# Four outputs at a time behind the norms of a two-block transformer kernel: four PSUM banks, weights in slices of two rows of tiles, and a re-timed norm chain

## The chip, the cores and the metric

The kernel runs on 1 core of one Trainium2 chip. The metric is the device time of one execution in microseconds (us). Before the change three runs gave 2636.99, 2637.52 and 2639.55 us, so the median is 2637.52 us.

## The reference, cut to what matters

Two transformer blocks of two layers each work on one sequence of 512 tokens with 1024 channels, in fp32. The change touches the second block only:

```python
def second_block(x, ...):
    for i in range(2):                                    # DEPTH = 2
        h = rms_norm_2(x, attn_pre_norm[i])
        z = h @ w_in[i]                                   # 1024 -> 26 tiles of 128 columns and 8 gate columns
        ...                                               # dilated attention, convolution mixer, gated delta rule
        x = x + rms_norm_2(mix @ w_out[i], attn_post_norm[i])      # post norm 0
        h = rms_norm_2(x, ffn_pre_norm[i])
        f = (silu(h @ w_gate[i]) * (h @ w_up[i])) @ w_down[i]      # 2816 hidden = 22 tiles
        x = x + rms_norm_2(f, ffn_post_norm[i])                    # post norm 1
    return x

def rms_norm_2(x, gain):
    return x * rsqrt(mean(x * x, axis=-1) + 1e-6) * gain
```

So each post norm is followed at once by a pre norm and a product of the new `x` with a large weight.

## The kernel before, in words

All activations are held transposed: 128 channels on the partitions, 512 tokens along the free dimension, so `x` is 8 tiles of 128x512 (`x_sb`; KD = 8). A product of fp32 accuracy is made of three matmuls of a rounded type: every fp32 operand is split into a high part (`whi`, `h_hi`) and the rest (`wlo`, `h_lo`), and a tile of output sums `h_hi*whi + h_lo*whi + h_hi*wlo` over the 8 tiles k of the input, 24 matmuls of 128x128 by 128x512.

**Units, pairs and slots.** One output tile is a *unit*; two units are a *pair*. There are two weight slots, s = 0 and 1, each with a `raw`, a `whi` and a `wlo` buffer of 8 (or 11) tiles of 128x128, and one PSUM bank each (ACC = banks 0 and 1). For unit (v, s) the SP queue loads `raw[s]` (line 458) once `wlo` of the unit before in this slot has been made; ScalarE makes `whi[s]` (`hi_next`, line 1449) when the matmuls that used the old one are done; VectorE makes `wlo[s]` (`low`, line 2095); TensorE computes it (`unit`, line 622); VectorE empties the bank. Numbers in semaphores (`w_hi_ready`, `w_lo_ready`, `unit_done`, `acc_free`) count the units of the whole program. The order on each engine is the order in which the code is written; nothing is scheduled by a planner.

**A post norm** (`post_norm` on ScalarE and VectorE, `post_parts` on GpSimd). The last pair of the output product leaves 8 tiles `y`. Their squares are summed on VectorE into `prod`, except the last, which stays in `cv1`; TensorE sums both over the channels with a matrix of ones (lines 1398 and 1400). ScalarE loads the table for logarithm and exponential (line 1460), and makes 1/rms by `exp(-0.5*ln(...))` (lines 1453, 1456) into a PSUM bank. Then for each of the 8 tiles n: VectorE scales `y` (line 2773) and adds it to `x` (2776); ScalarE makes `h_hi = x*gain` (2017), and the square of `x` (2008); VectorE makes `h_lo` (2767) for tiles 0, 2, 4, 6, 7, and GpSimd (546) from a copy in `pad` (2015) for tiles 1, 3, 5. GpSimd also sums the squares (554). The pre norm's 1/rms (`rstd`) is not needed before the matmuls: it is applied to their outputs. So the next product can start with tile k = 0 as soon as that is there.

**The product behind it** is `stream_pair` (line 686): for each k it issues 3 matmuls for the output in slot 0 and 3 for the one in slot 1. Before k = 7 `post_norm_sum` (lines 708, 710, 712) sums the squares over the channels in three fp32 matmuls. Behind it come plain units again. It is used at three places: the first pair of the gate/up product behind post norm 0 in both layers, and the first pair of layer 1's in-projection behind post norm 1 of layer 0. Layer 0's in-projection, behind the last product of the first block, uses `first_pair` (line 641). Post norm 1 of layer 1 is the end of the program; its tiles are turned (1428) and stored.

In the in-projection VectorE empties a bank with `project(i)` (2405), and turns outputs 0 to 3 by position with `rotary(i)` (2445 to 2448), for which TensorE makes a partner (`partners`, 1017).

## Time and profile before

| what | value |
|---|---|
| median of 3 runs | 2637.52 us (2636.99 to 2639.55) |
| the profiled execution | 2636.79 us, its span 2635.0 us |
| granted TensorE clock, mean | 0.989 of full |
| TensorE busy | 2551.0 us, 97% of the span |
| VectorE busy | 1514.5 us, 57% |
| ScalarE busy | 1105.3 us, 42% |
| GpSimd busy | 134.1 us, 5% |
| DMA | 208.04 MB, 79 GB/s in the mean |

The engines are PE (TensorE), PEld (its weight loads, which overlap PE), DVE (VectorE), ACT (ScalarE), POOL (GpSimd) and SP (the queue that issues most DMAs). A matmul's recorded length is longer than the distance to the next one, since matmuls are pipelined, so a busy PE can still be one that could do more; distances between starts tell its pace. A granted clock of 1.00 is TensorE's level of 2.4 GHz, 0.50 that of 1.2 GHz. "Idle before <-releaser" names what ended a wait.

### The profile page before, as it was taken

To read this page: it belongs to the slowest core of one execution; us is meant where nothing else is said; L and a number is where in the kernel's file an instruction comes from. 1 tells how busy PE (TensorE), PEld (TensorE's weight loads), DVE (VectorE), ACT (ScalarE), POOL (GpSimd) and SP (SyncE) were. 2 spreads that over 40 slices of the span, in tenths; PEclk is the share of its full clock that TensorE was granted. 3 is DMA by queue.
4 is the path that set the end of the run, shared out by engine and by line. 5 is a ranking of instruction groups with operands and counts; after the bars stand their busy time and mean duration, and the time that the engine had idled before them with its cause. 6 is when DMAs were issued, how large, how long until landed. Compare 5 with 4: busy or idle time off the path is not lost.

```text
span 2635.0 us, 36784 instructions
## 1 busy us (share of the span) xinstructions
PE 2551.0 (97%) x12956; PEld 2021.1 (77%) x12966; DVE 1514.5 (57%) x1957; ACT 1105.3 (42%) x1602; POOL 134.1 (5%) x119
## 2 busy tenths in 40 slices
PE   7999999999999999999998899999899999899998
PEld 5767888887668888887678778888676787688886
DVE  4656755756556746656975554344559755543444
ACT  4554433435554424432475443232424754431323
POOL 1000000000000000000212010000102120100000
PEclk9999999999999999999999999999999999999998
DMA  4203332333113333342220223333221201233333
GB/s 133 72 1 89 98 108 87 99 93 93 49 33 92 102 93 96 100 115 64 56 65 11 64 77 104 91 96 106 55 77 52 65 18 56 72 101 90 96 99 92
DMA packets 394592, 208.04 MB, mean 79 GB/s; under 512 B 9738, under 2 KB 392660, under 8 KB 394484
## 3 DMA queue, kind: packets, MB, share of 16 engines
q1 hardware_dynamic: 391396, 202.79, 26.7%
q0 software_dynamic: 2176, 3.06, 0.5%
q8 instruction: 65, 1.06, 0.2%
q10 hardware_dynamic: 912, 0.77, 0.1%
q14 instruction: 43, 0.35, 0.0%
...
## 4 chain that ended last, share of the span: by engine, by line
PE 89%; DVE 6%; ACT 3%; issue 1%; DMA 0%; SPq 0%; DVEq 0%; ACTq 0%
PE ps L622 65%; PE ps L641 6%; PE ps L899 2%; DVE ps L2773 1%; DVE x_sb L2776 1%; ACT whi L1449 1%; PE ps L1052 1%; PE ps L1067 1%; DVE yc L2497 1%; DVE h_lo L2767 1%; PE ps L1227 1%; PE ps L954 1%; PE ps L1205 1%; PE ps L956 1%; PE ps L955 1%
## 5 line engine op out<-in xcount | busy, mean ns | idle before, releaser
L1449 ACT ACTIVATE whi<-raw 128x1024 fp32r<-128x1024 f32 (+1 forms) x354 | 395.8, 1119 | 1071.2 <-PE ps L622 947.5
L622 PE MATMUL ps<-h_hi,whi 128*128 128x512 f32 x1984 | 789.2, 398 | 4.7 <-ACT whi L1449 4.1
L622 PE MATMUL ps<-h_lo,whi 128*128 128x512 f32 x1984 | 773.7, 390 | 0.0
L622 PE MATMUL ps<-h_hi,wlo 128*128 128x512 f32 x1984 | 530.3, 389 | 0.0
L2095 DVE TENSOR_TENSOR wlo<-raw,whi 128x1024 fp32r<-128x1024 f32 (+1 forms) x354 | 458.7, 1296 | 56.2 <-ACT whi L1449 55.1
L622 PEld LDWEIGHTS ps<-h_hi,whi 128*128 128x128 f32 x1984 | 373.3, 188 | 89.7 <-ACT whi L1449 8.2
L622 PEld LDWEIGHTS ps<-h_lo,whi 128*128 128x128 f32 x1984 | 373.2, 188 | 82.7 <-issue 6.2
L622 PEld LDWEIGHTS ps<-h_hi,wlo 128*128 128x128 f32 x1984 | 372.5, 188 | 77.2
L622 PE MATMUL ps<-a_hi,whi 128*128 128x512 f32 x592 | 230.3, 389 | 0.0
L622 PE MATMUL ps<-a_lo,whi 128*128 128x512 f32 x592 | 230.3, 389 | 0.0
L2808 DVE TENSOR_TENSOR cv<-ps,rstd 128x512 f32<-128x512 f32 x88 | 60.9, 692 | 248.9 <-PE ps L622 241.0
L622 PE MATMUL ps<-a_hi,wlo 128*128 128x512 f32 x592 | 152.4, 389 | 0.0
L2321 DVE TENSOR_TENSOR pad<-ps,rstd 128x512 f32<-128x512 f32 x88 | 61.0, 693 | 130.6 <-PE ps L622 118.4
L622 PEld LDWEIGHTS ps<-a_lo,whi 128*128 128x128 f32 x592 | 111.1, 188 | 23.1
L622 PEld LDWEIGHTS ps<-a_hi,wlo 128*128 128x128 f32 x592 | 111.1, 188 | 23.1
L622 PEld LDWEIGHTS ps<-a_hi,whi 128*128 128x128 f32 x592 | 111.1, 188 | 23.0
L2284 DVE TENSOR_TENSOR x_sb<-x_sb,ps 128x512 f32 (+1 forms) x40 | 27.5, 687 | 110.1 <-PE ps L622 94.1
L2330 DVE SCALAR_TENSOR_TENSOR cv<-pad,pc,cv 128x512 f32<-128x512 f32 x88 | 66.1, 751 | 11.0
L2497 DVE SCALAR_TENSOR_TENSOR yc<-ypad,pd,yc 128x512 f32<-128x512 f32 x88 | 70.4, 841 | 1.6
L1694 ACT ACTIVATE cv<-pad,pc,pb 128x512 f32<-128x512 f32 x88 | 70.5, 802 | 0.1
L1706 ACT ACTIVATE a_hi<-prod 128x512 f32 (+1 forms) x44 | 27.9, 633 | 97.8 <-DVE prod L2337 97.8
L641 PE MATMUL ps<-a_hi,whi 128*128 128x512 f32 x176 | 68.5, 389 | 0.0
...
## 6 DMA issues: line engine op xcount, KB each, us to landing
...
```

What stands on the lines that cost most here:

```text
L622: return pe.matmul(ps[:, ACC[s], :], w[s][:, k, :], r[:, k, :], start=start, stop=stop)
L641: return pe.matmul(ps[:, ACC[s], :], w[s][:, k, :], r[:, k, :], start=start, stop=stop)
L899: pe.matmul(ps[:, TRN[h % 2], :], vaug[:, h // GROUP, h % 2, kt, :], probs[:, kt, :], start=(kt == 0), stop=(kt == TB - 1)).then_inc(PV_do ...
L1449: act.activation(whi[s][:, 0:kt, :], raw[s][:, 0:kt, :], ACT.Copy).then_inc(w_hi_ready.sem, 1)
L1694: act.activation(cv[s][:], pad[s][:, 1:SEQ + 1], ACT.Identity, scale=param(pb, L, 2 * NF + col), bias=param(pc, L, 2 * NF + col))\
L1706: act.activation(tile(a_hi, j), prod[:], ACT.Copy).then_inc(ahi_ready.sem, 1)
L2095: dve.tensor_tensor(wlo[s][:, 0:kt, :], raw[s][:, 0:kt, :], whi[s][:, 0:kt, :].bitcast(F32), ALU.subtract).then_inc(w_lo_ready.sem, 1)
L2284: dve.tensor_tensor(tile(x, n), tile(x, n), ps[:, ACC[s], :], ALU.add).then_inc(acc_free.sem, 1)
L2321: dve.tensor_tensor(pad[s][:, 1:SEQ + 1], ps[:, ACC[s], :], rstd[:], ALU.mult).then_inc(acc_free.sem, 1)
L2330: dve.scalar_tensor_tensor(cv[s][:], pad[s][:, 2:SEQ + 2], param(pc, L, col), cv[s][:], ALU.mult, ALU.add)\
L2497: ins = dve.scalar_tensor_tensor(yc[:, t, :], src, w, yc[:, t, :], ALU.mult, ALU.add)
L2808: dve.tensor_tensor(cv[s][:], ps[:, ACC[s], :], rstd[:], ALU.mult).then_inc(acc_free.sem, 1)
```

## The change

`wide_pairs` takes the place of `stream_pair` at its three places and of `first_pair` in layer 0's in-projection. It computes four outputs at once in the PSUM banks WIDE = ACC[0], ACC[1], TRN[1], STAT[1], that is the work of two pairs: for each k 12 matmuls instead of 6. A slot's 8 tiles of 128 columns then hold 2 input tiles k by 4 outputs instead of 8 input tiles by 1 output: slot 0 holds k = 0, 1, slot 1 k = 2, 3, then slot 0 is refilled with k = 4, 5 and slot 1 with k = 6, 7. The refills fall into the post norm: on ScalarE behind tiles 3 and 6, on VectorE behind tile 5 and at the end, followed by the cast of the next pair's slot 0. Loads are changed to match: for the in-projection one DMA a slot, for gate and up two, of which ScalarE waits for the first with a semaphore of its own.

The chain of the post norm is changed too. In post norm 0 the table load is left out (the table in place holds the functions), and the last square is read from PSUM instead of from `y`, the copy waiting for it. In post norm 1 the table load is moved ahead of the last square. VectorE makes `h_lo` of tile 0 before it adds tile 1. GpSimd sums all 8 squares, so that one matmul instead of three makes the pre norm's sum, before k = 6 instead of k = 7.

Behind it, the first two pairs of gate/up have an epilogue of their own (`first_silus`, `first_pairs`), and in the in-projection four `project` stand together, followed by a cast and the two `rotary`; the two `partners` on TensorE follow the wide pairs.

```diff
+        WIDE = (ACC[0], ACC[1], TRN[1], STAT[1])
@@ SP: loads
+                    if off == OFF_UP2[0]:
+                        for k in range(0, KD, 2):
+                            load_wide(BASE2 + L * PAIRS2 + off + k // 4, (k // 2) % 2,
+                                      two_keys(wv["w_gate_2"], L, k, 2), two_keys(wv["w_up_2"], L, k, 2))
+                        pairs(2, n)
+                    elif off == 0:
+                        for k in range(0, KD, 2):
+                            load_wide(BASE2 + L * PAIRS2 + k // 4, (k // 2) % 2, two_keys(wv["w_in_2"], L, k, 4))
...
@@ GpSimd: post_parts
                 post_square_sum(p, 5)
+                post_square_sum(p, 6)
+                post_square_sum(p, 7)
@@ TensorE
+            def wide_pairs(v, wait_rhs, before, columns, done):
+                for k in range(KD):
+                    slot, pair = (k // 2) % 2, v + k // 4
+                    before(k)
+                    if k == 0:
+                        pe.wait_ge(acc_free.sem, v * 2 + 2)
+                    if k % 2 == 0:
+                        pe.wait_ge(w_lo_ready.sem, pair * 2 + (slot + 3))
+                    wait_rhs(k, 0)
+                    for o in range(4):
+                        bank, w = ps[:, WIDE[o], :], 4 * (k % 2) + columns[o]
+                        pe.matmul(bank, whi[slot][:, w, :], h_hi[:, k, :], start=k == 0, stop=False)
+                        pe.matmul(bank, whi[slot][:, w, :], h_lo[:, k, :], start=False, stop=False)
+                        mm = pe.matmul(bank, wlo[slot][:, w, :], h_hi[:, k, :], start=False, stop=k == KD - 1)
+                        if k == KD - 1 and o < 3:
+                            mm.then_inc(done.sem, 1)
+                    if k % 2 == 1:
+                        mm.then_inc(unit_done.sem, 1)
             def post_norm_sum(p):
-                pe.wait_ge(pssq_done.sem, pssq_done.at(p, KD - 4))
-                pe.matmul(ps[:, STAT[0], :], ones[:], ssq[:], start=True, stop=False)
-                pe.wait_ge(psq_ready.sem, psq_ready.at(p, KD - 2))
-                pe.matmul(ps[:, STAT[0], :], ones[:], sqt[:, 0, :], start=False, stop=False)
-                pe.wait_ge(psq_ready.sem, psq_ready.at(p, KD - 1))
-                pe.matmul(ps[:, STAT[0], :], ones[:], sqt[:, 1, :], start=False, stop=True).then_inc(stat_ready.sem, 1)
+                pe.wait_ge(pssq_done.sem, pssq_done.at(p, KD - 2))
+                pe.matmul(ps[:, STAT[0], :], ones[:], ssq[:], start=True, stop=True).then_inc(stat_ready.sem, 1)
...
-                stream_pair(V + OFF_UP2[0], h_hi, h_lo, need_post(2 * L), lambda k: k == KD - 1 and post_norm_sum(2 * L))
+                wide_pairs(V + OFF_UP2[0], need_post(2 * L), lambda k: k == KD - 2 and post_norm_sum(2 * L), (0, 2, 1, 3), wide_up)
@@ ScalarE: last_post_squares
-                    post_square(i, v, PAIRS_O - 1, 1)
+                    if i == 1:
+                        logs_and_exps()
+                    if i == 0:
+                        act.wait_ge(unit_done.sem, v * 2 + 4)
+                        act.wait_ge(yssq_done.sem, yssq_done.at(L, KD - 3))
+                        act.activation(cv[1][:], ps[:, ACC[1], :], ACT.Square).then_inc(ysq_ready.sem, 1)
+                        gates_in(0, 1)
+                    else:
+                        post_square(i, v, PAIRS_O - 1, 1)
                     hi_next(v + 1, 1, KD)
                 def post_rstd(i):
-                    logs_and_exps()
@@ ScalarE: post_norm
+                        if n == 3:
+                            wide_high(v + 1, 0)
+                        if n == 6:
+                            wide_high(v + 1, 1)
+                    hi_next(v + 2, 0, KD)
+                    act.wait_ge(stat_ready.sem, stat_ready.at(gen, 0))
+                    order.settle()
+                    order.told(rs(rstd[:], ps[:, STAT[0], :], DM), rstd_ready, gen, 0)
@@ VectorE: post_norm
+                        if more and n == 1:
+                            post_low(0)
                         order.settle()
                         order.told(dve.tensor_tensor(x[:, n, :], x[:, n, :], scaled, ALU.add), x2_ready, L, i * KD + n)
-                        if more and n - 1 in LOW_DVE:
+                        if more and n > 1 and n - 1 in LOW_DVE:
                             post_low(n - 1)
+                        if more and n == 5:
+                            low(v + 1, 0, KD)
                     if more:
                         post_low(KD - 1)
+                        low(v + 1, 1, KD)
+                        low(v + 2, 0, KD)
```

On ScalarE, at the end of the output product before post norm 0, this stood in a row before (`cv0`, `cv1` are the squares of the last two tiles of `y`, `whi0` and `whi1` the next weights):

```order
L1449 ACTIVATE whi0<-raw0 128x1024
L1977 ACTIVATE cv0<-y_sb 128x512
L1977 ACTIVATE cv1<-y_sb 128x512
L1449 ACTIVATE whi1<-raw1 128x1024
L1460 ACT_TABLE_LOAD
L1453 ACTIVATE lnt<-ps,eps 128x512
L1456 ACTIVATE ps<-lnt 128x512
```

and this stands there now:

```order
L1487 ACTIVATE whi0<-raw0 128x1024
L2019 ACTIVATE cv0<-y_sb 128x512
L2041 ACTIVATE cv1<-ps 128x512
L1487 ACTIVATE whi1<-raw1 128x1024
L1491 ACTIVATE lnt<-ps,eps 128x512
L1494 ACTIVATE ps<-lnt 128x512
```

The table load is gone, and the last square reads PSUM; the cast into `whi1` still stands between that square and the logarithm.

On VectorE, from tile 4 to the end of post norm 0, this stood in a row before:

```order
L2773 SCALAR_TENSOR_TENSOR ps<-y_sb,gains,ps 128x512
L2776 TENSOR_TENSOR x_sb<-x_sb,ps 128x512
L2767 SCALAR_TENSOR_TENSOR h_lo<-x_sb,gains,h_hi 128x512
L2773 SCALAR_TENSOR_TENSOR ps<-y_sb,gains,ps 128x512
L2776 TENSOR_TENSOR x_sb<-x_sb,ps 128x512
L2773 SCALAR_TENSOR_TENSOR ps<-y_sb,gains,ps 128x512
L2776 TENSOR_TENSOR x_sb<-x_sb,ps 128x512
L2767 SCALAR_TENSOR_TENSOR h_lo<-x_sb,gains,h_hi 128x512 x2
L62 ISA
L2808 TENSOR_TENSOR cv0<-ps,rstd 128x512
```

and from the same point (the add of tile 5 with its `h_lo` of tile 4) this stands there now:

```order
L2877 TENSOR_TENSOR x_sb<-x_sb,ps 128x512
L2866 SCALAR_TENSOR_TENSOR h_lo<-x_sb,gains,h_hi 128x512
L2180 TENSOR_TENSOR wlo0<-raw0,whi0 128x1024
L2872 SCALAR_TENSOR_TENSOR ps<-y_sb,gains,ps 128x512
L2877 TENSOR_TENSOR x_sb<-x_sb,ps 128x512
L2872 SCALAR_TENSOR_TENSOR ps<-y_sb,gains,ps 128x512
L2877 TENSOR_TENSOR x_sb<-x_sb,ps 128x512
L2866 SCALAR_TENSOR_TENSOR h_lo<-x_sb,gains,h_hi 128x512 x2
L2180 TENSOR_TENSOR wlo1<-raw1,whi1 128x1024
L2180 TENSOR_TENSOR wlo0<-raw0,whi0 128x1024
L62 ISA
L2944 TENSOR_TENSOR cv0<-ps,rstd 128x512
```

The refill of slot 0 stands in the middle of the norm, that of slot 1 and the cast for the unit behind the wide pairs at its end.

On TensorE, around the sum of squares for the pre norm, this stood in a row before (behind k = 6, ahead of k = 7):

```order
L686 MATMUL ps<-h_hi,wlo0 128x512
L686 MATMUL ps<-h_hi,whi1 128x512
L686 MATMUL ps<-h_lo,whi1 128x512
L708 MATMUL ps<-ssq,ones 128x512
L710 MATMUL ps<-sqt,ones 128x512
L712 MATMUL ps<-sqt,ones 128x512
L686 MATMUL ps<-h_hi,whi0 128x512
```

and this stands there now (behind k = 5, ahead of k = 6):

```order
L740 MATMUL ps<-h_hi,whi0 128x512
L741 MATMUL ps<-h_lo,whi0 128x512
L742 MATMUL ps<-h_hi,wlo0 128x512
L751 MATMUL ps<-ssq,ones 128x512
L740 MATMUL ps<-h_hi,whi1 128x512
L741 MATMUL ps<-h_lo,whi1 128x512
```

One sum took the place of three, and 24 matmuls from slot 1 (k = 6 and 7) stand behind it.

## Rows read from the trace of the kernel before

**Rows 1.** Waits of PE, whole run: total us, times, longest us
```profile
PE ps L686 <- DVE h_lo L2767: 19.5, 6, 6.1
```

**Rows 2.** Chain that ended last: start us, us, engine, tile, line
```profile
940.82 164.56 PE ps L622 x726
```

**Rows 3.** Timeline of PE, post norm 0 of layer 0: start us, us
```profile
1505.49 1.12 PE L1400 MATMUL ps<-cv,ones 128*128 128x512 f32 x2 [0.59 <-ACT cv L1977]
...
1512.73 0.80 PE L686 MATMUL ps<-h_hi,whi 128*128 128x512 f32 x1 [6.11 <-DVE h_lo L2767]
...
1526.66 1.02 PE L708 MATMUL ps<-ssq,ones 128*128 128x512 f32 x2
1527.52 1.02 PE L710 MATMUL ps<-sqt,ones 128*128 128x512 f32 x2
...
1532.12 0.50 PE L622 MATMUL ps<-h_hi,whi 128*128 128x512 f32 x1 [0.89 <-ACT whi L1449]
```

**Rows 4.** Timeline of ACT, the same stretch
```profile
1504.81 0.63 ACT L1977 ACTIVATE cv<-y_sb 128x512 f32<-128x512 f32 x1 [4.53 <-DVE y_sb L2744]
1505.35 1.04 ACT L1449 ACTIVATE whi<-raw 128x1024 fp32r<-128x1024 f32 x1
1506.40 1.28 ACT L1460 ACT_TABLE_LOAD   x1
1507.70 0.69 ACT L1453 ACTIVATE lnt<-ps,eps 128x512 f32<-128x512 f32 x1
...
1510.66 0.72 ACT L2017 ACTIVATE h_hi<-x_sb,gains 128x512 fp32r<-128x512 f32 x1 [1.64 <-DVE x_sb L2776]
```

**Rows 5.** Timeline of DVE, the same stretch
```profile
1504.09 0.69 DVE L2744 COPY y_sb<-ps 128x512 f32<-128x512 f32 x1 [1.94 <-PE ps L622]
...
1511.93 0.74 DVE L2767 SCALAR_TENSOR_TENSOR h_lo<-x_sb,gains,h_hi 128x512 fp32r<-128x512 f32 x1
...
1521.08 0.74 DVE L2773 SCALAR_TENSOR_TENSOR ps<-y_sb,gains,ps 128x512 f32<-128x512 f32 x1
```

**Rows 6.** PE by stretches: us, busy (instructions), granted clock, DMA share, GB/s
```profile
1516.00:1517.00 1.00, 1.00 (x5) 0.72 0.00 0
1895.00:1896.00 1.00, 1.00 (x5) 0.78 0.00 0
```

**Rows 7.** Lines 2767, 2095, 554: count, duration ns min/median/max, first and last start
```profile
L2767 DVE SCALAR_TENSOR_TENSOR h_lo<-x_sb,gains,h_hi x15: 744/1222/1891, 1511.9 to 2259.8; 128x512 fp32r<-128x512 f32 x15
L2095 DVE TENSOR_TENSOR wlo<-raw,whi x354: 1160/1219/2192, 12.4 to 2616.6; 128x1024 fp32r<-128x1024 f32 x145, 128x1408 fp32r<-128x1408 f32 x32
L554 POOL TENSOR_TENSOR ssq<-ssq,sqt x12: 1275/1293/1560, 1516.8 to 2257.1; 128x512 f32<-128x512 f32 x12
```

**Rows 8.** Timelines of PE, then ACT: post norm 1 of layer 0
```profile
1882.02 1.13 PE L1400 MATMUL ps<-cv,ones 128*128 128x512 f32 x2 [0.58 <-ACT cv L1977]
1889.26 0.80 PE L686 MATMUL ps<-h_hi,whi 128*128 128x512 f32 x1 [6.11 <-DVE h_lo L2767]
...
1909.55 0.47 PE L622 MATMUL ps<-h_hi,whi 128*128 128x512 f32 x1 [1.74 <-ACT whi L1449]
...
1884.23 0.69 ACT L1453 ACTIVATE lnt<-ps,eps 128x512 f32<-128x512 f32 x1
```

**Rows 9.** Timeline of PE: post norm 0 of layer 1
```profile
2246.36 0.79 PE L686 MATMUL ps<-h_hi,whi 128*128 128x512 f32 x1 [6.11 <-DVE h_lo L2767]
...
2265.75 0.50 PE L622 MATMUL ps<-h_hi,whi 128*128 128x512 f32 x1 [0.89 <-ACT whi L1449]
```

**Rows 10.** Timeline of PE: layer 0's in-projection
```profile
1165.05 0.39 PE L641 MATMUL ps<-h_hi,whi 128*128 128x512 f32 x1
...
1177.59 0.47 PE L622 MATMUL ps<-h_hi,whi 128*128 128x512 f32 x1 [0.59 <-issue]
```

**Rows 11.** All engines by stretches: layer 1's in-projection (third busy figure: DVE)
```profile
1947.00:1957.00 10.00, 9.75 (x42) 7.48 (x42) 4.70 (x8) 1.87 (x3) 0.00 (x0) 1.00 0.39 103
1967.00:1977.00 10.00, 10.00 (x43) 6.79 (x42) 9.65 (x16) 2.44 (x5) 0.06 (x1) 1.00 0.20 52
```

137 lines of the change are left out of this document (106 added, 31 removed).

## The prediction, as it was made before the changed kernel ran

> **What bounds the kernel now.** I read the page first: TensorE is busy for 97% of the span and most of the chain of waits is TensorE's line 622, so time can only come from stretches in which TensorE waits, runs slowly or computes what could be left out. I read the list of its waits next: by far the first is line 686, the pair behind a post norm, waiting for `h_lo` from VectorE, 19.5 us in six waits, the longest 6.1 us [rows 1]. Then I read the timelines around the norms. At its usual pace TensorE starts a matmul of a unit every 164.56/726 = 0.2267 us [rows 2]; a unit is 24 of them (5.44 us), a pair 10.88 us, two pairs 21.76 us. In post norm 0 of layer 0 the pair starts at 1512.73 and the next unit at 1532.12 [rows 3]: 19.39 us for 10.88 us of work. The places behind post norm 1 of layer 0 (1889.26 to 1909.55) and post norm 0 of layer 1 (2246.36 to 2265.75) take 20.29 and 19.39 us for the same work [rows 8, 9]. A tile of `x` takes longer to come than the six matmuls that it feeds.
>
> Where do the 8.51 us of the first place go? The granted clock is 0.72 from 1516 to 1517, that is 0.50 (1.2 GHz) until 1516.56 and then 1.00 (2.4 GHz) [rows 6]; before that TensorE had idled 6.11 us [rows 3]. So it ran 3.83 us at half pace, which loses 1.92 us. Three fp32 sums take 0.86 us each (1526.66 to 1527.52) [rows 3], 2.58 us. The last wait is 0.89 us for the cast `whi` [rows 3]. The rest, about 3.1 us, are waits for single tiles. Behind post norm 1 the clock comes back at 1895.44 (0.78 in that microsecond) [rows 6], 6.18 us after the start, and loses 3.09 us. I take the first place's loss for layer 1's post norm 0, whose interval is the same.
>
> **The wide pairs.** Twelve matmuls a tile k are 2.72 us at full clock. VectorE makes a tile of `x` with two instructions, about 0.74 and 0.7 us, and mostly one `h_lo`, 0.74 us at least [rows 5, 7]: 2.2 us. So tiles should come faster than TensorE uses them, and both pairs run without waiting except where a slot is refilled. At full pace the wide pairs cost 21.76 us, plus the half-clock loss, plus one fp32 sum, 0.86 us. The next unit's cast is then made one sum and 24 matmuls before it is needed.
>
> **When they start.** In post norm 0 the logarithm starts at 1507.70. Without the table load (1.28 us) it waits for the later of the cast (1505.35 + 1.04 = 1506.39) and the sum over the squares (1505.49 + 1.12 = 1506.61) [rows 3, 4]. That sum itself comes earlier: the square started at 1504.81 behind a copy that started at 1504.09, and now starts in the copy's place, 0.72 us earlier [rows 4, 5]. So the sum ends at 1505.89, the cast at 1505.67, the logarithm starts at 1505.93: 1.77 us earlier. The `h_lo` of tile 0 started at 1511.93 behind the add of tile 1, while `h_hi` was there at 1510.66 + 0.72 = 1511.38; moved ahead of the add it starts 0.51 us earlier [rows 4, 5]. Start of the wide pairs: 1512.73 - 2.28 = 1510.45. In post norm 1 only the table load moves: the logarithm goes from 1884.23 to 1882.02 + 1.13 + 0.04 = 1883.19 [rows 8], 1.04 us, with the 0.51 us 1.55 us; start at 1887.71. The table load now stands between two squares that are a unit apart, under TensorE's matmuls.
>
> **The refills.** Call e the moment at which k = 1 is done: 24 matmuls and the clock loss behind the start. ScalarE then casts (1.04) and makes `h_hi` of tile 4 (0.72), VectorE makes its `h_lo` (0.74) and `wlo` (1.22) [rows 4, 5, 7]; with four hand-overs of 0.05 us that is e + 3.9. TensorE wants slot 0 at e + 5.44, so it has 1.5 us to spare. The second refill is tighter. VectorE is free from e + 3.9, needs 2*(0.74 + 0.69) for tiles 6 and 7, of which tile 6 is there at e + 5.4; then ScalarE makes `h_hi` and the square of 6 (0.72, 0.63), casts (1.04), makes the square and `h_hi` of 7 (0.63, 0.72) [rows 4], VectorE `h_lo` of 7 (0.74) and `wlo` (1.22): e + 11.1, or + 11.3 with the hand-overs. TensorE wants it at e + 10.88 + 0.86 = e + 11.74. The sum before it needs the square of 7 (about e + 8.6) and one GpSimd add (1.29) [rows 7]: e + 9.9, in time. So by undisturbed lengths both refills are just hidden.
>
> They won't be undisturbed. `h_lo` takes 744 ns at best, 1222 ns in the middle and 1891 ns at most, and `wlo` up to 2192 where it mostly takes 1219 [rows 7]; the long ones stand where GpSimd's adds run, and there are now ten such operations in a norm instead of eight. The Trainium skill says why ("SBUF — State Buffer", Who interferes with whom): a VectorE instruction with two inputs in SBUF contends with a GpSimd instruction that reads SBUF, since both read through one shared interface. The trace agrees, by the stretched lengths just read. By that rule each of the two `wlo` casts in the norm may wait for a whole GpSimd add of 1.29 us, 2.6 us less the 0.4 us to spare, so 2.2 us a norm: that is the first rival. The sum goes by the lengths in the rows: nothing stretched gives no stall; `h_lo` of 4 and 6 and both `wlo` stretched to their longest would be 2*1.15 + 2*0.97 = 4.2 us, less the 0.4 us to spare, 3.8 us. I take 1.0 us a norm, nearer to the low end, because the middle `h_lo` is stretched by 0.48 us only.
>
> **The sum.** What counts is the time at which two pairs are done.
> - Post norm 0, layer 0: before 1532.12 + 10.88 = 1543.00; after 1510.45 + 21.76 + 1.92 + 0.86 + 1.0 = 1535.99. Gain 7.0 us.
> - Post norm 1, layer 0: before 1909.55 + 10.88 = 1920.43; after 1887.71 + 21.76 + 3.09 + 0.86 + 1.0 = 1914.42. Gain 6.0 us. The two partner matmuls stand on both sides.
> - Post norm 0, layer 1: before 2265.75 + 10.88 = 2276.63; after 2244.08 + 25.54 = 2269.62. Gain 7.0 us.
> - Layer 0's in-projection: before 1165.05 to 1177.59, 12.54 us, and 10.88 us, 23.42 us [rows 10]; after 21.76 + 0.86 = 22.62 us. There is no norm in its way and its casts have 5.44 us each. Gain 0.8 us, at most the same, at least -2 if a refill is late there too.
> - The last norm has no wide pair, but its table load moves too. Gain 1.0 us, as in post norm 1.
> Together 21.8 us. The profiled execution took 2636.79 us, which gives 2615.0 us; the median is 0.73 us above it, which gives 2615.7 us.
>
> **Edits that I cost at nothing.** Loads: the second DMA of a gate/up slot is issued on SP, which waits for VectorE anyway, long before the cast. The burst behind the wide pairs: the first bank is complete 9 matmuls (2.0 us) before their end and `rstd` some 4 us before, so VectorE frees ACC[0] before the next unit wants it; the other three banks, a cast and two rotaries are about 9 us of VectorE beside a unit, a partner and the gate columns. If that cover is gone, a unit waits up to 2 us, once a place. In the in-projection VectorE is busy for 4.70 of 10 us (1947 to 1957) before it fills at 9.65 of 10 (1967 to 1977) [rows 11], so it catches up before that.
>
> **Rivals.**
> 1. *The refills stall.* The casts stretched by GpSimd's adds, and ScalarE and VectorE waiting for each other around k = 3, make both refills late, 3 us a norm instead of 1. Speaks for it: the tight second refill and the stretched rows 7. Against: TensorE's slack of 0.5 us a tile builds up. Three norms at 2 us more: 2615.7 + 6 = 2622 us.
> 2. *No stall, and a shorter half-clock stretch.* TensorE idles 2.3 us less before the pair. With no stall (3.0 us) and the long stretch of post norm 1 as short as the others (1.2 us): 2611.5 us.
> 3. *The in-projection gives it back.* VectorE's full stretch [rows 11] is on the path; if its start is set by VectorE's own backlog and not by TensorE, the gains of both in-projections (6.0 + 0.8) are lost: 2622.5 us. Against: VectorE waits for TensorE in the stretch before.
> 4. *Slower: the half clock stays.* TensorE starts right after its idle time with the clock at 0.50. If twelve matmuls a tile did not bring it back, the whole of the wide pairs would run at half pace: 21.76 - 1.92 us more at three places, 60 us, less 21.8: 2675 us. It decides from 7.3 us more loss a place, 14.6 us longer at 0.50. Against: with gaps between the tiles the clock came back after 3.83 and 6.18 us; now there are fewer gaps.
> That the change does not do what it says I rule out by the order: the table load, the two sums and the refills are where the text puts them.
>
> **How the numbers follow.** My forecast 50%, rival 1 18%, rival 2 19%, rival 3 9%, rival 4 2%, and 2% for another loss that takes all, half of it "same", half slower. Reaching from the stall-free case to the middle of rivals 1 and 3 leaves out about 2 in 10: 2610 to 2622 us. Less than 0.2% (5 us) is about what a measurement can't tell from no change; all cases but the last two are faster by more than that, 96%, of which I give 2% to "same" for gains too small to see: faster 0.94, same 0.03, slower 0.03.
>
> **What would show it.** Right: between the start of the wide pairs and the next unit about 25.5 us behind a post norm 0, with waits only before k = 4 and k = 6; the logarithm 1.8 (post norm 0) and 1.0 us (post norm 1) earlier; no wait of TensorE for `whi` behind the norm; one sum of 0.86 us. Wrong: a wait before any odd k or of more than 2 us in one place; a granted clock of 0.50 for more than 8 us; a new wait in the in-projection behind the partners; VectorE idle before its full stretch there no shorter but TensorE waiting for it.

## The result, and the profile after

The changed kernel takes 2618.36 us (median of 4 runs, 2616.38 to 2619.01), the kernel before beside it 2638.53 us (2636.99 to 2639.64): ratio 0.9922, 95% interval 0.9910 to 0.9935. That is 20.2 us; 2615.7 was forecast. The profiled execution took 2618.87 us, its span is 2616.5 us (before: 2635.0), so 18.5 us are to be found between the two traces.

TensorE's list of waits in the changed kernel first (total us, times, longest us):

```profile
PE ps L740 <- DVE h_lo L2866: 13.9, 3, 4.7
PE ps L740 <- DVE wlo L2180: 1.7, 3, 0.6
PE ps L751 <- POOL ssq L575: 0.3, 1, 0.3
```

Line 740 is the first matmul of the wide pairs. The waits for `h_lo` have gone from 19.5 us in six to 13.9 us in three [rows 1]: one ahead of each wide group, none between tiles. New are three waits of 0.56 us for `wlo`.

The timeline of PE in post norm 0 of layer 0, as in [rows 3] (start us, us, engine, line, operation, idle before it and what ended it):

```profile
1505.88 1.02 PE L1436 MATMUL ps<-prod,ones 128*128 128x512 f32 x2
1506.73 1.12 PE L1438 MATMUL ps<-cv,ones 128*128 128x512 f32 x2
1512.50 0.77 PE L740 MATMUL ps<-h_hi,whi 128*128 128x512 f32 x1 [4.65 <-DVE h_lo L2866]
...
1531.88 1.13 PE L751 MATMUL ps<-ssq,ones 128*128 128x512 f32 x2
1533.56 0.50 PE L740 MATMUL ps<-h_hi,whi 128*128 128x512 f32 x1 [0.56 <-DVE wlo L2180]
...
1539.17 0.39 PE L645 MATMUL ps<-h_hi,whi 128*128 128x512 f32 x1
```

From the first fp32 sum (line 1436) to the next unit's first matmul, with both pairs done, it is 33.29 us. In the kernel before that stretch was 39.25 us (1503.89 to 1543.14). The wide group alone, 1512.50 to 1539.17, takes 26.67 us.

ScalarE in the same stretch, against [rows 4]:

```profile
1506.07 0.60 ACT L2041 ACTIVATE cv<-ps 128x512 f32<-128x512 f32 x1 [3.78 <-PE ps L645]
1506.57 1.05 ACT L1487 ACTIVATE whi<-raw 128x1024 fp32r<-128x1024 f32 x1
1507.89 0.69 ACT L1491 ACTIVATE lnt<-ps,eps 128x512 f32<-128x512 f32 x1 [0.27 <-PE ps L1438]
...
1517.56 0.63 ACT L2062 ACTIVATE sqt<-x_sb 128x512 f32<-128x512 f32 x1 [2.11 <-POOL ssq L575]
...
1521.10 1.06 ACT L1487 ACTIVATE whi<-raw 128x1024 fp32r<-128x1024 f32 x1 [1.16 <-PE ps L742]
1522.07 0.70 ACT L2076 ACTIVATE h_hi<-x_sb,gains 128x512 fp32r<-128x512 f32 x1
...
1527.22 0.72 ACT L2076 ACTIVATE h_hi<-x_sb,gains 128x512 fp32r<-128x512 f32 x1 [2.18 <-DVE x_sb L2877]
```

The logarithm (line 1491) starts 2.01 us behind the first sum, where it was 3.81 us behind it: 1.80 us earlier. Then ScalarE waits 2.11 us for GpSimd ahead of a square and 1.16 us for TensorE ahead of the cast for k = 4, and `h_hi` of tile 4 starts only at 1522.07. VectorE, against [rows 5]:

```profile
1511.60 0.75 DVE L2866 SCALAR_TENSOR_TENSOR h_lo<-x_sb,gains,h_hi 128x512 fp32r<-128x512 f32 x1
...
1522.81 0.75 DVE L2866 SCALAR_TENSOR_TENSOR h_lo<-x_sb,gains,h_hi 128x512 fp32r<-128x512 f32 x1 [3.64 <-ACT h_hi L2076]
1523.48 2.32 DVE L2180 TENSOR_TENSOR wlo<-raw,whi 128x1024 fp32r<-128x1024 f32 x1
1525.72 0.74 DVE L2872 SCALAR_TENSOR_TENSOR ps<-y_sb,gains,ps 128x512 f32<-128x512 f32 x1
...
1530.58 1.79 DVE L2866 SCALAR_TENSOR_TENSOR h_lo<-x_sb,gains,h_hi 128x512 fp32r<-128x512 f32 x1 [1.35 <-ACT h_hi L2076]
1532.30 2.35 DVE L2180 TENSOR_TENSOR wlo<-raw,whi 128x1024 fp32r<-128x1024 f32 x2
```

It is idle for 3.64 us ahead of `h_lo` (4), while the scale and add of tile 6 (from 1525.72), which need nothing from ScalarE, stand behind it in the queue. The first cast takes 2.32 us and `h_lo` (7) 1.79 us. So the cast for k = 6 (the first of the two at 1532.30) ends at about 1533.5, which is what TensorE waits for at 1533.56. GpSimd beside the first cast:

```profile
1523.37 1.34 POOL L575 TENSOR_TENSOR ssq<-ssq,sqt 128x512 f32<-128x512 f32 x1 [1.27 <-ACT sqt L2062]
1524.67 2.28 POOL L567 TENSOR_TENSOR h_lo<-pad,h_hi 128x512 fp32r<-128x512 f32 x1
```

GpSimd's addition ends at 1524.71, VectorE's cast 1.09 us later at 1525.80, and GpSimd's `h_lo` 1.15 us after that at 1526.95. So each of the two long ones ends about its own undisturbed length (1.22 and 1.29 us) behind the instruction that was running on the other engine.

TensorE's clock by stretches (us, busy, granted clock, DMA share, GB/s), where it comes back behind the three norms, against [rows 6]:

```profile
1518.00:1519.00 1.00, 1.00 (x4) 0.79 0.00 0
1887.00:1888.00 1.00, 1.00 (x6) 0.97 0.00 0
2238.00:2239.00 1.00, 1.00 (x5) 0.69 0.00 0
```

With 0.50 in the microseconds before, that is 5.9, 3.2 and 5.9 us at 1.2 GHz from the start of the group: longer than before in the first and third place (3.8 and 4.1 us), shorter in the second (6.2 us).

Post norm 1 of layer 0, PE and then ACT, against [rows 8]:

```profile
1883.83 0.77 PE L740 MATMUL ps<-h_hi,whi 128*128 128x512 f32 x1 [4.65 <-DVE h_lo L2866]
1902.32 1.12 PE L751 MATMUL ps<-ssq,ones 128*128 128x512 f32 x2 [0.29 <-POOL ssq L575]
1904.01 0.50 PE L740 MATMUL ps<-h_hi,whi 128*128 128x512 f32 x1 [0.56 <-DVE wlo L2180]
...
1879.22 0.69 ACT L1491 ACTIVATE lnt<-ps,eps 128x512 f32<-128x512 f32 x1 [0.27 <-PE ps L1438]
```

and post norm 0 of layer 1, against [rows 9]:

```profile
2232.72 0.77 PE L740 MATMUL ps<-h_hi,whi 128*128 128x512 f32 x1 [4.65 <-DVE h_lo L2866]
...
2253.77 0.50 PE L740 MATMUL ps<-h_hi,whi 128*128 128x512 f32 x1 [0.56 <-DVE wlo L2180]
...
2259.35 0.39 PE L645 MATMUL ps<-h_hi,whi 128*128 128x512 f32 x1
```

Layer 0's in-projection has a wait that it did not have before [rows 10]; the last matmul of the group ahead of it starts at 1165.44:

```profile
1166.61 0.50 PE L740 MATMUL ps<-h_hi,whi 128*128 128x512 f32 x1 [0.78 <-DVE x_sb L2369]
```

The budget, each stretch between the same two points of both traces: post norms 6.0, 7.0 and 6.0 us gained, last norm 1.1; layer 0's in-projection, from the last matmul ahead of it to the first unit behind its partners, 0.35 lost (25.08 us before, 25.43 now); the rest of layer 0 up to the first norm 1.0 lost, that of layer 1 0.4 gained; all that stands ahead of the in-projection 0.6 lost. That last stretch has the same code in every experiment on the changed kernel and ends anywhere from 1164.38 (e4) to 1166.42 us (e10), so the 0.6 us say nothing of the change. That is 18.5 us.

### The profile page after: what moved, and what is told of

It is laid out like the page before. It is cut to its first block, busy times and chain, and to the rows that moved or that the text cites. A ratio compares the mean times of both kernels' runs of the same rounds, so it can differ in the third digit from the quotient of the medians.

```text
span 2616.5 us, 36726 instructions
## 1 busy us (share of the span) xinstructions
PE 2547.0 (97%) x12954; PEld 2020.0 (77%) x12954; DVE 1514.3 (58%) x1957; ACT 1098.8 (42%) x1597; POOL 148.1 (6%) x125
## 4 chain that ended last, share of the span: by engine, by line
PE 89%; DVE 6%; ACT 3%; issue 1%; DMA 0%; POOL 0%; SPq 0%; DVEq 0%; ACTq 0%; POOLq 0%
PE ps L645 63%; PE ps L664 6%; PE ps L938 2%; PE ps L740 1%; PE ps L741 1%; PE ps L742 1%; PE ps L1089 1%; PE ps L1104 1%; DVE yc L2589 1%; PE ps L1265 1%; ACT whi L1487 1%; PE ps L1243 1%; PE ps L993 1%; PE ps L1285 1%; PE ps L995 1%
## 5 line engine op out<-in xcount | busy, mean ns | idle before, releaser
L645 PE MATMUL ps<-h_hi,whi 128*128 128x512 f32 x1920 | 763.7, 398 | 0.6 <-ACT whi L1487 0.6
L645 PE MATMUL ps<-h_lo,whi 128*128 128x512 f32 x1920 | 748.7, 390 | 0.0
L645 PE MATMUL ps<-h_hi,wlo 128*128 128x512 f32 x1920 | 513.2, 389 | 0.0
L645 PEld LDWEIGHTS ps<-h_hi,whi 128*128 128x128 f32 x1920 | 361.5, 188 | 81.4 <-ACT whi L1487 3.8
L645 PEld LDWEIGHTS ps<-h_lo,whi 128*128 128x128 f32 x1920 | 361.5, 188 | 79.8 <-issue 5.5
L645 PEld LDWEIGHTS ps<-h_hi,wlo 128*128 128x128 f32 x1920 | 360.5, 188 | 74.8
L645 PE MATMUL ps<-a_hi,whi 128*128 128x512 f32 x592 | 230.3, 389 | 0.0
L2913 DVE TENSOR_TENSOR cv<-ps,rstd 128x512 f32<-128x512 f32 x80 | 55.3, 692 | 227.6 <-PE ps L645 227.6
L740 PE MATMUL ps<-h_hi,whi 128*128 128x512 f32 x128 | 54.4, 425 | 16.4 <-DVE h_lo L2866 13.9
```

The lines of the kernel that those rows point to most:

```text
L645: return pe.matmul(ps[:, ACC[s], :], w[s][:, k, :], r[:, k, :], start=start, stop=stop)
L740: pe.matmul(bank, whi[slot][:, w, :], h_hi[:, k, :], start=k == 0, stop=False)
L2913: dve.tensor_tensor(cv[s][:], ps[:, ACC[s], :], rstd[:], ALU.mult).then_inc(acc_free.sem, 1)
```

## The experiments

Each experiment is one edit of the changed kernel (e2: of the kernel before), and the diffs are cut to the lines that count. All runs are read by the same four intervals: for each norm from the first fp32 sum of the `y` squares to the first matmul of the next unit (N0 and N1 of layer 0, N0 of layer 1), and from the last norm's first sum to the end of the span. They don't contain the stretches between the norms. Times in us; the ratio is to the kernel before in the same minutes.

| run | time, ratio (interval) | N0, N1, N0, last | sum |
|---|---|---|---|
| before | 2638.5 | 39.25, 41.49, 39.23, 20.96 | 140.9 |
| after | 2618.4, 0.9922 (0.9910 to 0.9935) | 33.29, 34.45, 33.25, 19.87 | 120.9 |
| after, again | 2617.4, 0.9921 (0.9907 to 0.9934) | 33.38, 34.46, 33.30, 19.94 | 121.1 |
| e1 wide only | 2623.7, 0.9947 (0.9934 to 0.9961) | 34.49, 35.92, 34.66, 20.95 | 126.0 |
| e2 chain only | 2632.4, 0.9983 (0.9974 to 0.9992) | 38.46, 41.18, 38.25, 19.89 | 137.8 |
| e3 VectorE order | 2613.2, 0.9914 (0.9900 to 0.9927) | 31.55, 34.28, 32.58, 19.88 | 118.3 |
| e4 five matmuls | 2615.8, 0.9917 (0.9903 to 0.9931) | 32.42, 34.46, 32.43, 19.94 | 119.3 |
| e5 no additions | 2612.6, 0.9906 (0.9891 to 0.9922) | 30.85, 32.83, 31.35, 19.93 | 115.0 |
| e6 = e3 + e4 | 2614.2, 0.9908 (0.9892 to 0.9923) | 31.58, 33.68, 31.56, 19.93 | 116.8 |
| e7 | 2614.1, 0.9909 (0.9893 to 0.9924) | 31.88, 33.94, 31.88, 19.85 | 117.6 |
| e8 own bank | 2615.0, 0.9916 (0.9902 to 0.9930) | 33.32, 34.46, 33.26, 19.89 | 120.9 |
| e9 high first | 2618.1, 0.9924 (0.9911 to 0.9938) | 32.43, 34.88, 33.66, 19.94 | 120.9 |
| e10 | 2620.1, 0.9932 (0.9919 to 0.9946) | 32.25, 35.94, 32.27, 19.87 | 120.3 |
| e12 = e6 + e8 | 2613.9, 0.9910 (0.9894 to 0.9927) | 31.59, 33.63, 31.60, 19.93 | 116.8 |

The timed intervals of everything from e3 on overlap with those of the changed kernel; what the edits do is read from the traces, one profiled execution for each run. The four intervals of the changed kernel's two traces agree within 0.1 us.

**The two parts of the change.** e1 puts the old chain back into the changed kernel:

```
 def post_rstd(i):
+    logs_and_exps()
 def last_post_squares(i, v):
-    if i == 1: logs_and_exps()
-    (i == 0: square of ACC[1], ahead of the drain)
+    post_square(i, v, PAIRS_O - 1, 1)
 VectorE: h_lo(0) behind the add of tile 1; the drain no longer waits for the square
```

> The changed kernel with the chain of the post norms as before: the table load back in front of the logarithm, the square of tile 7 again from y and behind the drain, h_lo of tile 0 again behind the add of tile 1. What is left is the four outputs at once. My theory: the two parts add up, but the 0.5 us of h_lo (0) is hidden, since the third quarter of the wide pairs waits for VectorE's last wlo anyway. The kernel loses against the changed one 1.8 us at each post norm 0, 1.0 at post norm 1 and 1.1 at the last norm, 5.7 in all: 2624.1, and the logarithm stands 3.8 us behind the first sum. Rival: the first matmul sets the end, so the whole 2.2 + 1.5 + 2.2 + 1.1 = 7.0 us come back: 2625.4. Rival: the chain was the whole gain, and this kernel is back at 2638.

5.2 us came back (126.0 against 120.9): the first theory's size, but not its mechanism. The group starts 2.3, 1.6 and 2.3 us later behind the first sum than in the changed kernel, the whole 7.3 us with the last norm's 1.1, and is itself 1.1, 0.1 and 0.9 us shorter. That isn't the stall: the wait ahead of k = 6 is 0.56 us in both. Behind the two post norms 0 it is the clock, for k = 0 to k = 1 takes 4.50 and 4.66 us here and 5.26 in the changed kernel. Behind post norm 1 the clock goes the other way (4.63 us here, 4.33 there), and the changed kernel's wait of 0.29 us for GpSimd ahead of the sum is missing here.

e2 is the opposite, the same three moves in the kernel before.

> The kernel before with the re-timed chain alone (table load ahead of the squares or gone, square of tile 7 from PSUM ahead of the drain in post norm 0, h_lo of tile 0 ahead of the add of tile 1); the pairs still run two outputs at a time. My theory: the logarithm comes 1.8, 1.0 and 1.8 us earlier, and 1.1 at the last norm; h_lo (0) gives nothing since the next tiles set the pace: 5.7 us in all, 2632.8. Rival: the early h_lo (0) delays every later tile by one VectorE operation of 0.75 us in a stream that waits for each tile: 5.7 - 3 x 0.75 = 3.5, 2635.0. Rival: it gains its whole 7.0: 2631.5.

3.1 us in the norms: 0.8, 0.3, 1.0 and 1.1 us. That is near the first rival, whose terms are 1.05, 0.3, 1.05 and 1.1, and its first step is in the trace: the add of tile 1 starts 6.40 us behind the first sum instead of 7.44, 1.04 us earlier and not 1.80, since `h_lo` (0) now stands ahead of it. It is not every later tile that is delayed, though (the add of tile 2 is 1.7 us earlier); what carries the delay on is GpSimd's queue. In e2, GpSimd and then TensorE:

```profile
1514.16 1.84 POOL L554 TENSOR_TENSOR ssq<-sqt 128x512 f32<-128x512 f32 x1
...
1519.35 0.50 PE L686 MATMUL ps<-h_hi,whi 128*128 128x512 f32 x1 [2.08 <-POOL h_lo L546]
...
1528.03 1.02 PE L712 MATMUL ps<-sqt,ones 128*128 128x512 f32 x2
```

GpSimd's first addition starts 1.05 us earlier than before, but takes 1.84 us instead of 1.27, so that its `h_lo` of tiles 3 and 5 comes only 0.48 and 0.31 us earlier, and TensorE waits for tile 3 (2.08 us; 0.54 before). The last square is not earlier at all (20.99 us behind the first sum before, 21.14 here), but nothing waits for it: it has ended at 1526.10, and the last fp32 sum starts at 1528.03 without a wait. Behind the wait of 2.08 us the clock fell once more, to 0.50 from 1521 to 1523.

The re-timed chain is worth 5.2 us beside the wide pairs and 3.1 us without them; the rest of the change 14.9 or 16.9 us of the 20.1. This rest is not the four outputs alone: GpSimd adds up the last two squares in e1 as well, and so one fp32 sum stands there in the place of three. Two sums of 0.86 us less at three places are 5.2 us by the rows of before, the waits for `whi` (0.89, 1.74 and 0.89 us [rows 3, 8, 9]) 3.5 us, and the waits for single tiles about 7.5 us (an estimate: k = 0 to k = 7 takes 16.96, 17.00 and 16.96 us before, less 42 matmuls, the clock and the sums). From these the new stall goes off, 3.3 us in e1, and about 1.4 us of half clock comes on. No run has the single sum without the four outputs.

**The stall ahead of k = 6.** e3 fills VectorE's idle time:

```
-    if more and n > 1 and n - 1 in LOW_DVE:
+    if more and n in (3, 7):
         post_low(n - 1)
-    if more and n == 5:
+    if more and n == 6:
+        post_low(4)
         low(v + 1, 0, KD)
```

> The changed kernel with one thing moved on VectorE: scale and add of tile 6 stand ahead of h_lo of tile 4 and of the wlo cast for k = 4, and fill the 3.6 us in which VectorE waits for h_hi of tile 4. My theory: the PE wait ahead of k = 6 (0.6 us for wlo, after 0.3 to 0.6 lost around the sum) is VectorE's queue; the last wlo comes 1.3 us earlier, the stall goes, and each of the three norms gains 0.6 to 1.1 us: 2.5 us in all, 2615.9. Rival: the stall is GpSimd's additions or ScalarE's whi cast, which do not move: 2618.4, with the wait ahead of k = 6 as it was. Rival: wlo for k = 4 comes later and stalls there: 2619.5.

The wait is gone at all three places, and the norms take 2.6 us less than in the changed kernel. VectorE in post norm 0 of layer 0:

```profile
1519.69 1.13 DVE L2866 SCALAR_TENSOR_TENSOR h_lo<-x_sb,gains,h_hi 128x512 fp32r<-128x512 f32 x1 [1.00 <-ACT h_hi L2076]
1520.74 2.32 DVE L2180 TENSOR_TENSOR wlo<-raw,whi 128x1024 fp32r<-128x1024 f32 x1
...
1527.63 3.63 DVE L2180 TENSOR_TENSOR wlo<-raw,whi 128x1024 fp32r<-128x1024 f32 x2
```

Idle 1.00 us instead of 3.64, and the casts for k = 6 and the next unit start 23.62 us behind the first sum (which is at 1504.01) instead of 26.42. Part of these 2.8 us is the clock, which came back 3 us sooner here; at the other two places the casts start 1.3 and 1.8 us earlier. From k = 5 to k = 6 it is now 4.03, 3.73 and 3.76 us, in the changed kernel 4.58, 4.86 and 4.59: 0.55 to 1.1 us of stall. Together that is 2.5 us. The rest of the difference between runs is the clock, which about cancels: half clock lasted 3.0, 5.4 and 6.1 us here and 5.9, 3.2 and 5.9 us in the changed kernel.

**What stretches the casts.** e5 leaves GpSimd's additions of tiles 2 to 7 out, so its sum of squares is not the right one:

```
 def post_square_sum(p, n):
-    nc.gpsimd.tensor_tensor(ssq, ..., sqt[:, n % 2, :], ALU.add).then_inc(pssq_done.sem, 1)
+    if n > 1: pool.sem_inc(pssq_done.sem, 1)    # tile 1 still adds
```

> The changed kernel without GpSimd's additions of the squares of x tiles 2 to 7 in the three norms (the sum holds tiles 0 and 1 only, so the result is scaled otherwise); their signals still go out at once, and GpSimd's three h_lo tiles stay. It asks why the wlo casts beside them take 2.3 us and not 1.2. My theory, contention of VectorE and GpSimd: both wlo casts in the norm fall back to 1.2 us and h_lo (4) and (7) to 0.75, ScalarE no longer waits 2.1 us for GpSimd ahead of a square, h_hi (4) and the last wlo come 3 us earlier, k = 5 to k = 6 falls from 4.6 us to 3.7: 0.9 us at each of the three norms, 2.7 in all against the changed kernel. Rival: the casts are long for another reason (the two slots' DMA writes land beside them), they stay at 2.3 us, and only the waits for GpSimd go: 1 us in all or less.

```profile
1519.75 0.75 DVE L2868 SCALAR_TENSOR_TENSOR h_lo<-x_sb,gains,h_hi 128x512 fp32r<-128x512 f32 x1 [2.39 <-ACT h_hi L2078]
1520.42 1.22 DVE L2182 TENSOR_TENSOR wlo<-raw,whi 128x1024 fp32r<-128x1024 f32 x1
...
1526.42 0.75 DVE L2868 SCALAR_TENSOR_TENSOR h_lo<-x_sb,gains,h_hi 128x512 fp32r<-128x512 f32 x1 [1.34 <-ACT h_hi L2078]
1527.09 1.22 DVE L2182 TENSOR_TENSOR wlo<-raw,whi 128x1024 fp32r<-128x1024 f32 x1
```

The cast is back at 1.22 us and `h_lo` (7) at 0.75 (2.32 and 1.79 above): the rival that the DMAs stretch them is out. The norms take 5.9 us less, twice what was expected. From k = 5 to k = 7 it is 6.35 us, where the changed kernel has 7.47, 7.73 and 7.45: 3.6 us in the three places are the additions'. e5 doesn't divide them: with the stretched lengths it also takes away ScalarE's waits for GpSimd ahead of the squares, and TensorE's 0.29 us in post norm 1. The other 2.3 us are the clock, which came back earlier in this run (k = 0 to k = 1 in 4.27, 4.17 and 4.75 us). GpSimd is held up as well: its `h_lo` (5), 2.28 us beside the cast, takes 1.29 us here. By the rule that the prediction cited (the Trainium skill, "SBUF — State Buffer", Who interferes with whom) this contention was to be expected, and this run shows it.

**The half clock.** e4 keeps TensorE busy between the sum and the group:

```
     pe.wait_ge(acc_free.sem, v * 2 + 2)
+    for _ in range(5):        # not in layer 0's in-projection
+        pe.matmul(ps[:, ACC[0], :], ones[:], prod[:], start=True, stop=True)
```

> The changed kernel with five fp32 matmuls (ones by the sum of squares, 0.86 us each) that nobody reads, on the bank of the first output, between the sum of the y squares and the first matmul of the wide pairs, at the three wide places behind a post norm; they fill 4.3 of TensorE's 4.65 us of waiting. My theory: the granted clock stays at 1.0 and the 3.0, 1.7 and 3.0 us of half clock go, but then k = 6 meets the last wlo, which VectorE ends at the same time as before but for the 1.2 us in which ScalarE waited for k = 1: the wait ahead of k = 6 grows to about 2.5 us, and the gain is 1.2 us a norm, 3.5 in all: 2614.9. Rival: half clock and stalls are independent: 7.7 us, 2610.7. Rival: the clock falls in spite of them (the product that gates is elsewhere), 2618.4; or they delay the first wide matmul, up to 1 us a place, 2621.

TensorE by stretches, from the five matmuls into the group, first and second place:

```profile
1506.00:1510.00 4.00, 4.00 (x10) 1.00 0.42 128
1510.00:1514.00 4.00, 3.33 (x14) 1.00 0.01 3
1877.00:1881.00 4.00, 3.65 (x9) 1.00 0.47 131
1881.00:1885.00 4.00, 3.65 (x15) 1.00 0.00 0
```

The clock stays at 1.00, so the loss of 2.9, 1.6 and 2.9 us comes from TensorE's idle time and can be avoided. What is gained is 1.6 us in all: the list of waits now has

```profile
PE ps L742 <- DVE wlo L2182: 3.7, 6, 0.7
```

These are six waits for `wlo` where there were three: k = 4 begins 0.8 us late as well as k = 6, and k = 1 waits 0.3 us for GpSimd's `h_lo`, which is the theory's mechanism and half of its size. In post norm 1 nothing is left of it.

e6 joins e3 and e4.

> The five unread matmuls of the fourth experiment and the VectorE order of the third together. Alone, the order gave 2.6 us within the norms by the trace and the matmuls 1.7. My theory: the stalls are what took the matmuls' gain, so together they give more than the sum 4.3: the clock stays at 1.0, k = 5 to k = 6 is 3.7 us, only the stall of 0.8 us at k = 4 is left (wlo ends at 1523.0 in both), and a wide part takes 24.6 us where the changed kernel has 26.7, 25.8 and 26.7: 5.4 us in all. Rival: the two only add, 4.3 us, or VectorE's queue bounds k = 6 again and k = 5 to k = 6 stays at 4.8: 2.5 us.

4.1 us less than the changed kernel, where e3 and e4 alone give 2.6 + 1.6: they add, and no more. k = 5 to k = 6 is 4.03 us at all three places, the stall at k = 4 stays (3.55 us from k = 3, 0.8 over the usual 2.72), and a group takes 24.95 us.

e7 tries to remove it by the order of VectorE, and has e8's wait:

```
     if more and n == 6:
-        post_low(4)
         low(v + 1, 0, KD)
+        post_low(4)
 if more:
-    post_low(KD - 1)
     low(v + 1, 1, KD)
+    post_low(KD - 1)
```

> The candidate for a better kernel: the five unread matmuls, scale and add of tile 6 ahead of the pair wlo cast for k = 4 and h_lo (4), in this order, the last wlo cast ahead of h_lo (7), and the first matmuls of a wide group wait for their own bank alone. My theory: the k = 4 stall shrinks from 0.8 to about 0.2 us, k = 5 to 6 is 3.7, each wide part takes 24.0 us (2.7, 1.8 and 2.7 less than in the changed kernel), and the layer 0 in-projection 0.9 less: 8 us less than the changed kernel, 0.9890 of the kernel before. Rival: h_lo (4) behind the cast of 2.3 us is late itself, and stalls k = 4 as long as before: 6.3 us less. Rival: h_lo (7) behind the last cast stalls k = 7: 5 us less or fewer.

3.3 us less than the changed kernel in the norms: both rivals together. k = 3 to k = 4 stays at 3.63 us, since now `h_lo` (4) runs beside GpSimd and takes 1.78 us behind a cast of 2.27, and k = 6 to k = 7 is 3.16 us instead of 2.89; the sum waits 0.5 us for GpSimd.

e9 asks whether ScalarE should stop standing behind GpSimd:

```
+    high(n)
+    if n == 4: wide_high(v + 1, 0)
+    if n > 0: square(n - 1)
     if n == 6: wide_high(v + 1, 1)
 + square(KD - 1) behind the loop; high(n) / square(n) in their old place go
```

> The changed kernel with ScalarE's order in the norms alone changed: h_hi of a tile stands ahead of the square of the tile before it, and the whi cast for k = 4 behind h_hi (4), so that no h_hi waits for GpSimd's additions through a square (2.1 us ahead of the third square, 1.2 to 2.4 ahead of the last). My theory: VectorE's wait of 3.6 us for h_hi (4) goes, both wlo casts come 1.5 to 3 us earlier, and k = 5 to k = 6 falls from 4.6 us to 3.7: 1.1 us less at each norm as in the third experiment, 3 in all against the changed kernel, and the sum ahead of k = 6 now waits up to 0.5 us for GpSimd. Rival: GpSimd's additions, one tile later, end after k = 5 and the sum ahead of k = 6 stalls by more than it gains: k = 5 to k = 6 at 4.6 us or more, no gain or up to 3 us a norm lost.

The rival: no gain. k = 5 to k = 6 takes 4.88, 4.51 and 4.53 us. The waits of the sum for GpSimd, 0.3 us once in the changed kernel, are

```profile
PE ps L751 <- POOL ssq L575: 3.6, 3, 1.4
```

e10 adds the five matmuls, the cast behind the add of tile 6 and e8's wait to it.

> The second candidate: ScalarE's order of the run before this one, the wlo cast for k = 4 behind the add of tile 6, the five unread matmuls, and each first matmul waits for its own bank. My theory: h_hi (4) no longer waits for GpSimd, so the stall of 0.8 us at k = 4 that was left with the unread matmuls goes; k = 0 to 1 3.3 us, k = 5 to 6 3.7, the rest 2.7 to 2.9: 24.0 us for a wide part, 2.7, 1.8 and 2.7 less than in the changed kernel, and 0.7 less in layer 0's in-projection: 7.9 us in all. Rival: GpSimd's queue bounds the sum ahead of k = 6, which waits 1 to 2 us there: 4 us in all. Rival: the additive 4.2 + 0.7 = 4.9 us of the parts measured so far.

The stall at k = 4 is gone (2.78 us from k = 3), as expected, and everything is paid at the sum, as the rival had it:

```profile
PE ps L755 <- POOL ssq L575: 5.6, 3, 1.9
```

GpSimd's queue of seven additions and three `h_lo` is the second bound, right behind VectorE's. In this run a group takes 25.7, 27.3 and 25.7 us. The 27.3 us behind post norm 1 are a clock fall: after the wait of 1.90 us ahead of the sum the clock was at 0.50 until 1908.4, and k = 6 to k = 7 took 4.66 us instead of 3.14. After the waits of 1.88 and 1.85 us at the other two places it stayed at 1.00.

**The in-projection.** e8 lets each output wait for its own bank:

```
-    if k == 0:
-        pe.wait_ge(acc_free.sem, v * 2 + 2)
     for o in range(4):
+        if k == 0 and o < 2:
+            pe.wait_ge(acc_free.sem, v * 2 + 1 + o)
```

> The changed kernel with the one wait of a wide group for both banks of the last pair split in two: the first output waits for its bank, the second for its own. My theory: layer 0's in-projection loses the wait of 0.78 us behind VectorE's add that the changed kernel has there, and the three places behind a norm, where the banks have long been free, do not move: the last unit's end to the first wide matmul falls from 1.17 us to 0.25, 0.9 us in all, which only the trace can tell from no change. Rival: the next wait (for wlo or for h of tile 0) stands right behind it and takes its place: no gain.

```profile
1165.15 0.39 PE L645 MATMUL ps<-a_hi,wlo 128*128 128x512 f32 x1
1165.38 0.39 PE L740 MATMUL ps<-h_hi,whi 128*128 128x512 f32 x1
...
1188.46 1.88 PE L1054 MATMUL ps<-za,perm 128*128 128x512 f32 x4
```

The list has no wait any more, and from the last matmul ahead of the group to the partners it is 23.31 us instead of 23.98 (1165.44 to 1189.42). 0.67 us are had, not 0.9, for the second output still starts 0.49 us behind the matmul before it where 0.23 is usual; at the norms nothing moves.

The gain doesn't hold in every kernel with the split wait. To the first unit behind the partners the changed kernel takes 25.43 us, e8 24.76, e12 24.78, e10 25.04, but e7 25.95, half a microsecond more. There ScalarE's cast of the third slice waited 6.54 us for its DMA and started at 1179.04 (1177.60 in e8, with its group at the same time), the later casts and the pre norm's 1/rms followed, and the partners waited 0.81 us for VectorE's `za`. So once the bank is no longer waited for, the landing of the weights is the next bound there.

**The stretches between the norms.** e11 is the changed kernel again.

> The changed kernel itself, unedited, beside the two: what the others are compared with in the same minutes, and how much one profiled execution of it differs from another. My theory: the norms keep their intervals of 33.3, 33.1 and 33.2 us within 0.1 but for TensorE's time at half clock, which moves by 1 us from run to run; the two stretches between layer 0's in-projection and the first norm and of layer 1 move by up to 1 us with the same clock at the start of the delta heads. Rival: they are fixed to 0.1 us, and the 1.1 us that layer 0's stretch lost came with the change.

TensorE by stretches in layer 0's delta heads, in the changed kernel's first trace and in the second:

```profile
1250.00:1254.00 4.00, 4.00 (x18) 1.00 0.00 0
1254.00:1258.00 4.00, 3.50 (x11) 0.70 0.48 131
1258.00:1262.00 4.00, 4.00 (x17) 0.87 0.00 0
```

```profile
1254.00:1258.00 4.00, 3.25 (x14) 1.00 0.48 131
1258.00:1262.00 4.00, 4.00 (x19) 1.00 0.00 0
```

The second trace has no clock fall there and takes 1.1 us less from the in-projection to the first norm: 315.6 us against 316.7 (from the last matmul of its group, at 1189.46 and 1189.18, to the first sum, at 1505.07 and 1505.88). The kernel before had no fall there either, and from the first unit behind the partners to the first sum it takes 313.98 us, the changed kernel 315.01 and 313.92. So the 1.0 us that the changed kernel seemed to lose is not of the change. A second fall, at 1430 to 1446, is in every trace and is 3.4 us (changed kernel) to 10 us long (e10); it was longer in the second trace (7 us) and gave back part of what the first fall cost, for directly behind that one the two traces are 1.56 us apart. The stretch was longest in e10, 319 us.

The other half of the theory did not hold: at the norms the time at half clock did not move by 1 us, but is 6.1, 3.3 and 6.0 us in the second trace, 5.9, 3.2 and 5.9 in the first.

e12 is the candidate: e3, e4 and e8 together.

> The three edits of which the traces showed a gain, together: the VectorE order of the third experiment, the five unread matmuls, and the first matmul of a wide group waiting for its own bank alone. My theory: they add, as the first two did: the intervals of the three norms are 31.6, 32.4 (1.9 less with the same end as before) and 31.6 us, 4.2 us less than in the changed kernel, and layer 0's in-projection 0.7 less: 4.9 us, 0.9903 of the kernel before. The stretch between them still moves by up to 3 us with TensorE's clock at two places in the delta heads. Rival: the earlier end of the in-projection is paid back by a clock fall in the delta heads (the two kernels with the split wait had one at 1254 to 1262 us): no more than 0.9910. Rival: the split wait lets the unread matmuls start before the second bank is free and the first wide matmul waits longer: an interval of 31.9 instead of 31.6.

The four intervals are those of e6, 4.1 us less than in the changed kernel, and the in-projection has no wait: 4.8 us by the trace. The ratio is 0.9910 (0.9894 to 0.9927), the number that the expectation named for the rival; this trace has the clock fall at 1254 to 1262 (0.78 and 0.79). It beats the kernel before; against the changed kernel (0.9922) the intervals of the timed runs overlap, so that it is faster than that one too rests on the traces. The single times agree with it: this kernel's four are 2613.52 to 2614.47 us, the changed kernel's nine, taken at other times, 2616.37 to 2619.01.

## Why the prediction was right, step by step

- **The wide pairs are limited by TensorE.** Right. From k = 1 on (full clock) a tile takes 2.72 us at every place, and there is no wait ahead of an odd k. The step carries most of the gain: 14.9 us in e1 against before, with the single sum in it.
- **When they start.** Right to 0.1 us: the first wide matmul stands 6.62, 7.37 and 6.62 us behind the first sum; the prediction's starts make 6.56, 7.29 and 6.55. The logarithm is 1.80 and 1.05 us earlier, 1.77 and 1.04 forecast.
- **The half clock.** Right in kind, off in size. I copied each place's loss from the trace of before (1.92, 3.09, 1.92 us); the group's excess ahead of k = 3 is 2.88, 1.64 and 2.86 us. In sum 7.4 against 6.9, so it is luck that the errors cancel: each place was wrong by 1 to 1.5 us, and that is where the three gains miss: 5.96, 7.04 and 5.98 us measured, 7.0, 6.0 and 7.0 forecast. The time at 1.2 GHz was no property of the place: in the first one it is 2.8 to 6.1 us behind the same idle time, from one kernel to another. e4 shows that the idle time is its cause; what sets its length stays open.
- **The refills and the sum.** 1.0 us of stall and 0.86 for the sum were forecast; from k = 5 to k = 7 the changed kernel takes 2.0, 2.3 and 2.0 us over two tiles. The first refill stretched and held: e, the end of k = 1, is 1520.8, and the cast ends at e + 5.0, forecast for e + 3.9 and wanted at e + 5.44. The second was forecast for e + 11.3 and wanted at e + 11.74; it came at e + 12.7. The two stretched instructions, the cast at 2.32 and `h_lo` (7) at 1.79 us, make VectorE's queue 2.1 us longer, and e5 shows who stretches them. The 1.0 us that I took was the right size. What stood in the order, and I had not seen, is that scale and add of tile 6, with their data ready, stood behind a wait of 3.64 us (e3).
- **Layer 0's in-projection, +0.8 us.** Failed: 0.35 us lost. I compared 23.42 with 22.62 us and did not count that the new group waits for both banks of the pair before, the old one for the first alone; the prediction sought a new wait behind the partners, and it stood ahead of the group. From the last matmul ahead to the group's first it is 1.17 us, 0.22 before. With e8 the term becomes a gain of 0.3 us (24.76 us against 25.08).
- **The last norm.** 1.09 us, 1.0 forecast. Here only the table load counts.
- **The rivals.** 1 (3 us of stall a norm, 2.2 by the cited rule) had the mechanism, but of the size only the 1.1 to 1.4 us a norm that e5 takes away. 2 was right on the second place's clock alone. 3 did not happen: the stretches between the norms are equal but for TensorE's clock falls. 4 did not happen: the clock is back within 6 us at every place.
- **The sum.** 21.8 us forecast, 20.2 us by the medians; the norms give 20.1 against 21.0. The two traces give 18.5 us where the medians give 20.2, so agreement within 1 to 2 us proves nothing.
